# First tile of expert rows gathered after four of eight selection rounds, and the last gate's rows computed inside the linear attention

## The reference, cut to what matters

```python
mod = silu(cond) @ w_ada + b_ada          # 6 parts: shift_a, scale_a, gate_a, shift_f, scale_f, gate_f
h = rmsnorm(x) * (1 + scale_a) + shift_a
y = token_mixer(h)                        # w_in, gated linear attention and pooling, w_out
x = x + gate_a * y
h = rmsnorm(x) * (1 + scale_f) + shift_f
probs = softmax(h @ w_router)             # per token, 16 experts
gate_vals, tok_idx = top_k(probs.T, 2 * n // 16)      # 64 latent and 16 context tokens per expert
xe = take(h, tok_idx)
ye = (silu(xe @ w_e_gate) * (xe @ w_e_up)) @ w_e_down * gate_vals
x = x + gate_f * scatter_add(ye)
```

## Time and profile before

| | us |
|---|---|
| three runs, median (lowest to highest) | 1740.54 (1737.47 to 1741.93) |
| the profiled execution, device time | 1739.62 |
| its span, first to last instruction | 1737.5 |
| PE busy in the span | 1672.4 (96%) |
| DVE, ACT, POOL busy | 375.6, 185.3, 135.3 |
| mean granted TensorE clock | 0.982 |
| DMA, mean over the span | 362 GB/s |

### The profile page before, as it was taken

The page is one execution under the profiler, slowest core; times in us unless marked ns, Lnnn a source line. Parts: engine busy times, 40 slices in busy tenths (PEclk is TensorE's granted clock), DMA queues, the critical chain, the costliest instruction groups (busy, mean ns, idle before and its releaser), DMA issues.

```text
span 1737.5 us, 43008 instructions
## 1 busy us (share of the span) xinstructions
PE 1672.4 (96%) x19754; PEld 1036.3 (60%) x19754; DVE 375.6 (22%) x695; ACT 185.3 (11%) x295; POOL 135.3 (8%) x204
## 2 busy tenths in 40 slices
PE   6998879799999999999999999999999999999997
PEld 3787558433434356666666666666668787444443
DVE  5431573611111102020202020202020111111113
ACT  4331451200000000000000000000000000000001
POOL 1000020120101010101000000000000001010000
PEclk9999989799999999999999999999999999999999
DMA  8620842999999999999999999999999999999995
GB/s 314 218 79 1 301 150 108 366 389 416 407 417 408 416 408 417 408 416 408 416 408 415 410 410 414 400 416 399 412 403 412 396 416 398 419 399 418 395 418 243
DMA packets 123341, 628.22 MB, mean 362 GB/s; under 512 B 11197, under 2 KB 14098, under 8 KB 106794
## 3 DMA queue, kind: packets, MB, share of 16 engines
q1 hardware_dynamic: 111872, 598.74, 85.3%
q0 software_dynamic: 10256, 23.91, 4.7%
q10 hardware_dynamic: 1050, 2.97, 0.4%
HBM read 609.37 MB, written 16.21 MB: 360 GB/s over the span
## 4 chain that ended last, share of the span: by engine, by line
PE 87%; DMA 6%; DVE 3%; ACT 1%; issue 1%; SPq 1%; ACTq 0%; DVEq 0%; POOLq 0%
PE bank L1782 48%; PE bank L1794 17%; PE bank L1796 8%; DMA ring<-in_w_e_up 3%; PE bank L1369 3%; PE bank L1370 3%; PE bank L1371 3%; DMA ring<-in_w_e_gate 1%; PE bank L1396 1%; SPq L444 1%; PE bank L1681 1%; DMA raw<-in_w_out 0%; PE bank L1391 0%; DMA pos_col<-in_pos 0%; DVE S L1093 0%
## 5 line engine op out<-in xcount | busy, mean ns | idle before, releaser
L1782 PE MATMUL bank<-ring,xe 128*32 128x352 f32 x12288 | 917.6, 460 | 5.2 <-DVE xe L1293 3.1
L1782 PEld LDWEIGHTS bank<-ring,xe 128*32 128x32 f32 x12288 | 557.7, 110 | 359.4 <-issue 160.9
L1794 PE MATMUL bank<-ring,hidT 128*32 128x512 f32 x2816 | 385.5, 592 | 0.0
L1796 PE MATMUL bank<-ring,hidT 128*32 128x256 f32 x2816 | 235.4, 379 | 0.0
L1796 PEld LDWEIGHTS bank<-ring,hidT 128*32 128x32 f32 x2816 | 129.5, 110 | 172.6 <-issue 172.6
L1300 DVE TENSOR_TENSOR hid<-sg,bank 128x1056 f32<-128x1056 f32 x32 | 40.1, 1255 | 829.9 <-PE bank L1782 829.9
L1794 PEld LDWEIGHTS bank<-ring,hidT 128*32 128x32 f32 x2816 | 127.4, 110 | 29.3 <-issue 2.5
L881 ACT ACT_TABLE_LOAD x16 | 20.5, 1283 | 867.4 <-PE bank L1782 867.4
L643 POOL DMA_INDIRECT acc_dram<-yab,idx_s x15 | 24.3, 1622 | 1028.9 <-DVE yc L1311 1028.9
L1309 DVE SCALAR_TENSOR_TENSOR yab<-bank,gate_cur,gfab 128x512 f32<-128x512 f32 x16 | 12.0, 751 | 330.4 <-PE bank L1796 330.4
L881 ACT ACTIVATE sg<-bank 128x1056 f32<-128x1056 f32 x32 | 33.6, 1051 | 420.6 <-PE bank L1782 420.5
(11 more groups left out here) (262 smaller groups left out, 772.3 us busy)
## 6 DMA issues: line engine op xcount, KB each, us to landing
ring<-in_w_e_gate SPq DMA_DIRECT2D x128, 1408.0 KB, 25.2
ring<-in_w_e_up SPq DMA_DIRECT2D x128, 1408.0 KB, 25.0
ring<-in_w_e_down SPq DMA_DIRECT2D x96, 1536.0 KB
ring<-in_w_e_down SPq DMA_DIRECT2D x32, 1024.0 KB
raw<-in_w_ada SPq DMA_DIRECT2D x16, 1024.0 KB, 6.2
raw<-in_w_in SPq DMA_DIRECT2D x8, 1024.0 KB, 5.5
ada_f<-in_w_ada SPq DMA_DIRECT2D x4, 1024.0 KB, 16.5
raw<-in_w_out SPq DMA_DIRECT2D x4, 1024.0 KB, 8.4
```

What stands on the lines that cost most here:

```text
L1782: last = nc.tensor.matmul(bank[b][32 * g:32 * g + 32, 0:GCOLS], xe[:, t, c, :], w[:, n, GCOLS * g:GCOLS * g + GCOLS], start=c == 0, stop=c ...
L1794: nc.tensor.matmul(bank[6][r:r + 32, :], hidT[:, ph, t, c, :], w[:, n, 512 * h:512 * h + 512], start=first, stop=stop)
L1796: last = nc.tensor.matmul(bank[7][32 * g:32 * g + 32, 0:256], hidT[:, ph, 2, c, :], w[:, n, 256 * g:256 * g + 256], start=first, stop=stop)
```

## The change: what it does

1. Blocks 10 and 11 of `w_ada` join `PRE`, behind block 9 and ahead of `w_out`: four more 1 MB loads. The 13 loads from block 5's second half on use six places of the split weights (`SPLIT_SLOTS`, `LATE_PLACES`, `ada_l`), free once the input projection is done, in place of the three slots.
2. PE makes both blocks just before `o_rows`, ACT copies them to `modrow`, and `o_rows` wait for both copies (`mod_row`, `ADA_BLOCKS + 1`). `ada_raw`, `gate_row` and both `gate_rows` go.
3. DVE writes tile 0's row numbers after round 3 and copies the turned index after round 4; POOL gathers tile 0 then. After round 7 DVE writes tile 1's row numbers and makes tile 0 ready for PE, ahead of the context rounds.
4. In the first expert PE runs tile 0 alone over units 0 to 7; the turning of tile 2's row numbers (`turn_rows(2, 4)`) stands ahead of unit 7. Then come the result tables (`turn_results`), then tiles 1 and 2 in pairs over units 0 to 7, with `unit_used` after tile 2.
5. Slot 11 moves to unit 5 in the ring's order, and the waits in `fill` move from units 7, 9, 11 to 8 and 10. Tile 2's gather waits for the context rows' own semaphore (`xn2_ctx`).

```diff
-PRE += [("ada", b, kh) for b in range(ADA_FIRST, ADA_SPLIT) for kh in range(2)]
+PRE += [("ada", b, kh) for b in range(ADA_FIRST, ADA_BLOCKS) for kh in range(2)]
+SPLIT_SLOTS = (3, 4, 5, 8, 9, 10)
+LATE_PLACES = (0, 1, 2, 3, 4, 5, 0, 1, 2, 4, 5, 1, 2)
-EXP_SLOTS = (0, 1, 8, 9, 10, 4, 7, 5, 6, 2, 3, 11)
+EXP_SLOTS = (0, 1, 8, 9, 10, 11, 4, 7, 5, 6, 2, 3)
...
+                    elif pre_slot(n) in SPLIT_SLOTS:
+                        sp.wait_ge(unit_used, split_count(split_user(pre_slot(n))))
...
                 elif n == 2:
-                    sp.wait_ge(wo_ps, 2 * T_LAT)
-                    for q in range(4):
-                        b, kh = divmod(q, 2)
-                        c0 = (ADA_SPLIT + b) * 512
-                        load(ada_raw[:, (q + 2) % 4, :].rearrange("p (k n) -> p k n", k=4), rows(w_ada[0, kh * 512:(kh + 1) * 512, c0:c0 + 512]), ada_in[q])
                     sp.wait_ge(unit_used, NSPLIT)
-                elif n == 7:
+                elif n == 8:
...
             nc.scalar.copy(mrows[:, :], bank[6][0:48, 0:P]).then_inc(mod_row, 1)
+            mod_rows(ADA_SPLIT)
+            mod_rows(ADA_SPLIT + 1)
             o_squares((0, 1))
...
+                if r == 3:
+                    dve.wait_ge(q_set, 4 + TOK - CAP_CTX)
+                    tile_rows_of(0)
+                if r == 4:
+                    tile_index(0)
+            tile_rows_of(1)
+            rows_tile(0, 0)
             dve.wait_ge(r_prT, 2)
...
+            for b in range(ADA_SPLIT, ADA_BLOCKS):
+                for kh in range(2):
+                    ada(b, kh)
             pe.wait_ge(scan_done, HP)
+            pe.wait_ge(mod_row, ADA_BLOCKS + 1)
             o_rows(0)
...
                 if first:
-                    for t in range(ROW_TILES):
-                        pe.wait_ge(xe_done, t + 1)
-                        for j in range(4):
-                            if t == 0:
-                                loaded(j, i)
+                    turn_rows(1, 2)
+                    pe.wait_ge(xe_done, 1)
+                    for j in range(8):
+                        if j == 4:
+                            pe.wait_ge(hid_done, 1)
+                        if j == 7:
+                            turn_rows(2, 4)
+                        loaded(j, i)
+                        into(j, 0)
+                    turn_results()
+                    pe.wait_ge(xe_done, 3)
+                    pe.wait_ge(idx_sb, 5)
+                    for j in range(8):
+                        if j == 4:
+                            pe.wait_ge(hid_done, 1)
+                        for t in range(1, ROW_TILES):
                             last = into(j, t)
-                            if t == ROW_TILES - 1:
-                                last.then_inc(unit_used, 1)
-                    pe.wait_ge(idx_sb, 4)
+                        last.then_inc(unit_used, 1)
```

More of the change, by code:

```diff
@@ L86, in pre_slot, with split_user @@
 def pre_slot(n):
-    return FRONT_SLOTS[n] if n < FRONT else (n - FRONT) % PRE_RING
+    if n < FRONT:
+        return FRONT_SLOTS[n]
+    if ADA0 + PRE_RING <= n < WOUT0:
+        return SPLIT_SLOTS[LATE_PLACES[n - ADA0 - PRE_RING]]
+    return (n - (FRONT if n < WOUT0 else WOUT0 - (ADA0 - FRONT))) % PRE_RING
 def pre_loads(slot, n):
     return sum(pre_slot(q) == slot for q in range(n))
+def split_user(slot):
+    return [n for n in range(ADA0) if PRE[n][0] == "win" and pre_split(n) == SPLIT_SLOTS.index(slot) % SPLIT][-1]
 def pre_last(slot):
@@ L226, in build @@
         ada_f = [at(f"ada_f{q}", [P, UNIT], F32, SPL + (q % 2 * SPLIT + q // 2) * UNIT * 4) for q in range(4)]
+        ada_l = [at(f"ada_l{q}", [P, UNIT], F32, SPL + q * UNIT * 4) for q in range(2 * SPLIT)]
         pos_col = at("pos_col", [P, 512], F32, SPL + 40 * KB)
@@ L316, in ada_unit, with pre_place @@
             return b - 1 if b < ADA_FIRST else ADA0 + 2 * (b - ADA_FIRST)
+        def pre_place(n):
+            slot = pre_slot(n)
+            return ada_l[SPLIT_SLOTS.index(slot)] if slot in SPLIT_SLOTS else raw[:, slot, :]
         def ada_count(b, kh):
@@ L325, in ada_bank @@
                 return bank[5 + place_of(b) % 2]
+            if b >= ADA_SPLIT:
+                return bank[3 if b == ADA_SPLIT else 0]
             return bank[1 + 2 * (b % 2)]
@@ L419, in ring_need @@
         def ring_need(j, i):
[L420 removed]
+            return 16 * (pre_loads(EXP_SLOTS[j % RING], NPRE) + j // RING + 1) + i * (16 * (EXP_UNITS // RING))
         def unit(j, i):
@@ L1760, in _ @@
-            last.then_inc(idx_ps, 1)
-            pe.wait_ge(grow_sb, 2)
-            pe.wait_ge(parts_set, 1)
-            for h in range(2):
-                last = nc.tensor.matmul(bank[6][64 * h:64 * h + 64, :], parts_of[:, LAT:LAT + 1].broadcast_to([P, 64]), gate_row[:, h, :], start=True, stop=True)
-            last.then_inc(gate_ps, 1)
-            for q in range(4):
-                last = nc.tensor.matmul(bank[7][32 * q:32 * q + 32, 0:256], parts_of[:, CTX:CTX + 1].broadcast_to([P, 32]),
-                                        gate_row[:, q // 2, q % 2 * 256:q % 2 * 256 + 256], start=True, stop=True)
@@ L1772, in loaded @@
+            turn_row(T_LAT)
+            turn_rows(0, 1)
+            logits(T_LAT)
+            turn_probs()
             def loaded(j, i):
```

152 lines of the change are left out of this document (71 added, 81 removed).

## The result

The changed kernel takes 1748.97 us (median of 6 runs, 1746.60 to 1751.80), the kernel before 1740.25 us in the runs beside it: ratio 1.0045, 95% interval 1.0033 to 1.0056, 7.8 us slower by the ratio and 8.7 by the medians. A second timing of both, made with experiment 7, gives 1.0058, which is 10.1 us, so the loss is known to about 2 us. The profiled executions are 1748.78 and 1739.62 us, 9.2 apart, with spans of 1747.0 and 1737.5.

What follows compares the result with a forecast made beforehand. The weight stream was taken to bound the kernel. Delay 4.8 + 2.5 + 0.2 - 1.5 = 6.0 us, plus 1.1 us of wider hole, made 7.1 us: forecast 1747.2 us, range 1737 to 1751.5.

Steps and rivals of the forecast that it cites:

- `w_out`'s load: Before the pooling: `w_out`'s first load, behind four more loads, lands at 214.2 instead of 209.4, 4.8 us later.
- my bound of 6: Upper bound on the delay of `w_out`'s first load: 6 us, from 3.4 us per load.
- Half clock in the pooling: After idling 9.9 us for `w_out`, TensorE pools and turns at half clock, costing 2.5 us more.
- Blocks 10 and 11 ahead of `o_rows`: Their products fill TensorE's wait for the scan; with copy and handover `o_rows` start 0.2 us later (0 to 1).
- Full clock in `o_rows`: TensorE no longer idles ahead of `o_rows`, so tile 0 runs at full clock, giving 1.5 us back (0 to 1.5).
- First tile: First expert: TensorE starts 10 us earlier but waits for tile 2; the weight stream's hole grows by 1.1 us, head start spent.
- The stream sets the end: Experts: the weight stream needs about 86.8 us per round against TensorE's 85.18, so it sets the end once the ring's lead is used.
- TensorE sets the end: Rival, experts: stream keeps 85.2 us per round, the 10 us head start carries through, 1733 us; chance 0.07.
- delay stays small: Rival: `w_out` lands only 3.4 us late and the clock holds through the pooling, 1743.5 us; chance 0.20.
- hole closed: Rival: delay as forecast, but tile 2's gather lands sooner and unit 0 is back by 360.4, 1744 us; chance 0.11.

Runs made afterwards that it cites:

- experiment 7: Changed kernel with extra identity products on TensorE during its wait for `w_out`'s load: 1749.14 us with 70 products; 1747.59 and 1745.91 us with 54.
- after_again: The changed kernel as it is, timed again beside the second run with 54 extra products: 1749.58 us, ratio 1.0058 to the kernel before.
- experiment 2: Changed kernel with tile 2's row numbers and the result tables turned behind three units instead of seven and eight: 1745.74 us, ratio 1.0034.
- experiment 4: Changed kernel with all three tiles turned, gathered and multiplied together after the eight rounds, blocks 10 and 11 staying moved: 1745.97 us, ratio 1.0032.
- experiment 5: Changed kernel with `w_out`'s first load ahead of blocks 10 and 11, and the three tiles together after the eight rounds: 1730.80 us, ratio 0.9941.
- experiment 6: Half of each down unit's columns not loaded for experts 1 to 15: changed kernel 1742.31 us, kernel before 1736.25 us.

## Why the prediction was right

Predicted were 1747.2 us and slower as the likeliest side; measured 1748.97. Step by step, by the profiled executions:

- **`w_out`'s load, predicted 4.8 us late:** ScalarE starts on it at 215.04 against 209.42, thus 5.6. The load took 11.7 us to land where I had 9.4, and it was issued 1.5 us earlier than I had forecast (203.30 against 204.8), which hid most of that.
  - The early issue is luck of this trace: in the second trace of the same kernel, of the run `after_again`, `w_out` goes out at 204.85, as forecast, and ScalarE starts at 216.78, 7.4 us late and past my bound of 6.
  - Of the 2.3 us that I had too little for the landing, 1.0 stands in block 11's first half, which landed 6.3 us after its issue and not 5.3. Its reason is in the first sentence of that step: I had block 10's loads out early, "their places come free with blocks 7 and 8", and counted two loads ahead of `w_out`. Block 8's products run at 198, so block 10's second load goes out at 199.15, in the same rush: three 1 MB loads ahead, all issued within the 4.1 us before `w_out`.
  - Another 1.2 us stand between block 11's second half (landed at 211.1) and `w_out` (215.0): 3.9 us, where I had put 2.7, though the kernel before shows 3.4 for the same step. Two bias loads of 128 KB, issued behind `w_out` from 204.05 on, land at about 213.2 and 213.7, ahead of it, and from 212 to 214 only 238 GB/s are moved; that they take this time from `w_out` is likely, but no run shows it.
  - The Trainium skill ("DMA: Bandwidth & Descriptors", section "Anatomy of one DMA — SWDGE (gpsimd) path") gives a DMA issued by GpSimd as about 2.0 us plus its bytes at 436 GB/s; the estimate by it was 212.7, where the rows gave 214.2 and the trace has 215.0.
- **Half clock in the pooling, predicted 2.5 us:** from `w_hi`'s start to `mod_columns(9)` it was 215.32 - 209.42 = 5.9 us, and is now 223.67 - 215.04 = 8.6: 2.7 us. Experiment 7 shows that the clock's share reaches the end; its 2.5 us are of the pooling and of later stretches together.
- **Blocks 10 and 11 ahead of `o_rows`, predicted 0.2 us:** from `mod_columns(9)` to `o_rows` 9.39 us before, 9.58 now. Right.
- **Full clock in `o_rows`, predicted 1.5 us back:** tile 0 took 3.98 us and takes 2.45. Right, but 1.3 us are lost 20 us later, which I had not followed up: I had "the rest up to the experts follows in order". TensorE waits 2.38 us ahead of L1728 where it waited 0.80, and the 16 transposes there run at half clock, 3.52 us for 2.19. So the delay is 7.0 us behind `o_rows`' first tile and 8.35 at the end of the output projection (327.29 against 318.94), where I had 6.0.
- **First tile, predicted 1.1 us of wider hole, head start spent:** 4.3 against 3.2 us of hole, and 1.2 of TensorE's 8.35 us recovered (7.15 at the second expert). Right in size, in part by luck. I had unit 0 given back 1.1 to 1.3 us later than the delay alone would have it; the refill goes out 8.33 us later than before, no more than the delay, since TensorE waits 4.64 us for tile 2 and not 6. The hole is wider all the same, because the loads ahead of it run out only 7 us later: the rate falls below 100 GB/s at 361.5 in the kernel before and at 368.5 in the changed one. Why they don't carry the whole delay is not shown. Experiments 2 and 4 add that the pass over eight units is what holds unit 0 back.
- **The stream sets the end:** right, by experiments 5 and 6, though 6.1 us of the loss would be there with a stream that doesn't limit.

The terms come to 8.35 + 1.1 = 9.4 us; the spans are 9.5 apart. That agreement is closer than the account deserves: the refill is 8.3 us later, the last expert's first activation 8.8 (1656.41 against 1647.65), and where the last 0.7 us come from is not shown. The shortfall of the forecast, 7.1 us for 9.4, is in the landing of `w_out` (0.8 net of the early issue) and, for the larger part, in the half clock at L1728.

Of the rivals, "TensorE sets the end" was wrong by experiment 6, "delay stays small" by the 12.27 us wait with half clock behind it, "hole closed" by the 4.3 us of hole.

## What to carry to other kernels

- Prefetches queued ahead of the load that the chain needs next can cost that load their transfer times: 11.7 us to land behind three loads of its size, 5.1 with none ahead (the load issued at 199.15). Sort a queue by when each load is needed, not by when its place comes free: one moved line in SP's order was worth 14 us here, and turned a loss of 8 us into a gain of 6.
- With a ring of weights whose stream is the bound, ask of each order of the first products when it gives the first unit back. An early start that keeps units for a second pass can widen the hole that it was to close; 5 us of head start on TensorE were worth nothing, a closed hole 2 to 3 us.
- Price each longer wait of TensorE twice, as the wait and as the half-clock work behind it, and follow where a faster piece makes the next wait longer.

## What the runs showed of the hardware

- The granted clock was 1.00 from 206 to 208, with TensorE idle since 205.2, and 0.50 from 210 to 222, the last 4.5 us of it unbroken work. The length of a wait alone doesn't tell what follows: 2.38 us ahead of L1728 was followed by half clock (3.52 us for 16 transposes; 2.42 us and 3.55 in a second trace), the 2.35 us in the earlier trace rows by full clock.
- A half-clock stretch need not be answered by less waiting: products of no use in the wait kept the clock at 1.00 and gave 2.5 us back.
- Loads of one queue need not land in the order of their issue: `w_out`'s 1 MB, issued at 203.30, landed at 215.0, and a bias load of 128 KB issued behind it at 204.05 landed at about 213.2.
- Executions of one kernel differ by 1.5 us already in the first 202 us (block 9 at 200.91 in the changed kernel's first trace and at 202.45 in its second, of the run `after_again`), so that a time read from one trace as absolute is good to some 2 us only; distances within these two traces agreed to 0.3 us (32.3 and 32.6 us from block 9 to `o_rows`).
